# Two gated feed-forward branches: the hidden activations turned by 32x32 transposes on VectorE and 16 small transfers per block instead of by TensorE transposes

## The chip, the cores and the metric

The program runs on one core of one Trainium2 chip. The metric is the device time of one execution in microseconds (us); of several executions the median is given. "Engines" below are TensorE (PE in the rows; PEld is its weight load), VectorE (DVE), ScalarE (ACT), GpSimd (POOL) and SyncE (SP), which here only issues transfers.

## The reference, cut to what matters

One layer on x of 256 rows x 2048 columns, float32. Two gated feed-forward branches stand around a mixer; the change touches only the branches:

```python
def swiglu(h, w_gate, w_up, w_down):
    return (jax.nn.silu(h @ w_gate) * (h @ w_up)) @ w_down

h = modulate(rmsnorm(x, g_ffn1_pre[l]), sh1, sc1)
y = rmsnorm(swiglu(h, w1_gate[l], w1_up[l], w1_down[l]), g_ffn1_post[l])
x = x + MACARON_WEIGHT * gt1[:, None, :] * y
...
h = modulate(rmsnorm(x, g_mix_pre[l]), sh2, sc2)
y = hybrid_mixer(h, pos, ...)
x = x + gt2[:, None, :] * rmsnorm(y, g_mix_post[l])
...
```

The second branch is the same with its own weights. w_gate and w_up are 2048 x 5632, w_down is 5632 x 2048. The shifts, scales and gates (`sh1`, `sc1`, `gt1`, ...) are columns of `silu(c) @ w_ada + b_ada`, a matrix of 2048 x 18432 that is read once.

## The kernel before, in words

**Tiling.** The 256 rows are two tiles of 128 (`TT`). Every product is made with a float32r high part and a float32r low part of both factors: three matmuls (high by high, high by low, low by high; lines 1460 to 1462) for one. A *unit* is two 128-row chunks of a weight times 512 columns (512 KB): SP loads it into one of 8 `raw` buffers (line 430), ACT rounds it to `w_hi` (one of 4 buffers, line 565), DVE subtracts to `w_lo`, in the place of `raw` (line 924), and PE makes 12 matmuls of it.

**Gate and up.** The 5632 hidden columns are 11 blocks of 512 (`FB`). In a block PE makes 8 units of the gate and 8 of up, each into a PSUM pair. ACT takes silu of the gate into `s` (line 657), DVE multiplies `s` by the up product in place (`hidden`, line 1104). The down product contracts over hidden columns, so `s` has to be turned: PE makes eight 128x128 transposes in two fills of `tps` (`turn_s`, line 1543), behind unit 2 of the next block; ACT rounds each fill to `hid_hi` (`hi_hid`, line 663), DVE subtracts to `hid_lo` (`lo_hid`, line 1110). PE takes `hid_hi` and `hid_lo` only in the down product, after all blocks.

**The first four blocks of branch 1.** While the modulation columns come in, their products are built in four turns, and partial sums are kept. Only the last turn ends the blocks, so there a block has 4 units of PE work, not 16. ACT puts a partial sum back ahead of each product (`put_back`, line 731).

**Order.** Each engine has its program written out by hand: a loop over the units of a block, with the other work put in front of a given unit. In branch 1 DVE also adds up `w_ada` between the units (line 938), 12 instructions in a block of 16 units. Before the change the later blocks of the gate and up stand in hardware loops (`Fori`); `RUNS` says which. A `Fori` of several rounds there is in branch 2 alone (blocks 6 to 10).

**Waits.** ACT rounds unit u only when PE is done with unit u-4 (4 `w_hi` buffers). SP loads into a `raw` buffer when PE (a weight) or DVE (a piece of `w_ada`) is done with what lay there. In the short blocks ACT rounds two units ahead of the one at PE. GpSimd does nothing but four memsets at the start.

Of the kernel before, what the change touches and what calls it, by code (L numbers as in the profile page):

```python
# [24 lines left out]
ALU = mybir.AluOpType  # L25
ACT = mybir.ActivationFunctionType
# [93 lines left out]
def make_plan():  # L120
# [34 lines left out]
    for f in ("1", "2"):  # L155

        fills("mod" + f, 8 if f == "1" else 4, "a" if f == "1" else "va")
        fills("hid" + f, 2 * (FB - 1), "v")
        fills("gate" + f, 4, "a")
        fills("hidlast" + f, 2, "v")  # L160
# [12 lines left out]
def build(nc, A, const, out):  # L173
    pl, tp, taken, order = make_plan()
    ctx = ExitStack()
    with ctx:
# [87 lines left out]


# [41 lines left out]
        setup = sem("setup")  # L307

# [32 lines left out]
        def landed(r, i=0, per=0):  # L341

            extra = sum(q <= r and q % RING == r % RING for q in doubled)
            return 16 * (r // RING + 1 + extra) + (i * (16 * per // RING) if per else 0)

        def plus(n, i, per):

            return n + i * per if per else n
# [11 lines left out]
        for k, n in (("mod1", 8), ("hid1", 2 * FB), ("modmix", 8), ("qa", 2), ("kv", 1), ("mod2", 8), ("hid2", 2 * FB)):  # L360
            TH[k] = n_th
            n_th += n
# [4 lines left out]
        RUNS = {"gu1": [(b, 1) for b in range(OPEN_FF, FB)], "gu2": [(b, 1) for b in range(1, 6)] + [(6, FB - 6)]}  # L367
# [45 lines left out]

        block = ctx.enter_context(nc.Block())
# [3 lines left out]
        def _(sp):  # L418
            ada = A["w_ada"].rearrange("(p j) (q n) -> p j q n", j=KD, n=NB)

            def load(r, src, n=NB, i=0, per=0, per_w=0):

                if r >= RING:
                    before = r - RING
                    assert not per or order[before:r] == order[before + per:r + per]
                    if order[before] == "W":
                        sp.wait_ge(w_used, plus(order[:before + 1].count("W"), i, per_w))
                    else:
                        sp.wait_ge(raw_used, plus(before + 1, i, per))
                sp.dma_start(raw[:, r % RING, :, 0:n], src).then_inc(raw_landed[r % RING], 16)  # L430

            def stream(b, unit, i=0, per=0, per_w=0):

                for n, (kind, u) in enumerate(b.seq):
                    if kind == "W":
                        src, cols = unit(u)
                        load(b.r + n, src, cols, i, per, per_w)
# [46 lines left out]
            for f, gu, down in (("1", "gu1", "down1"), ("2", "gu2", "down2")):  # L484
# [6 lines left out]
                for start, count in RUNS[gu]:  # L491
                    b = pl[gu][start]
                    if count == 1:
                        stream(b, gate_up(wg, wu, start))
                        continue
                    with sp.Fori(0, count) as i:
                        stream(b, gate_up(wg, wu, i + start), i, len(b.seq), 16)
# [55 lines left out]

        @block.scalar
        def _(act):
            def hi_unit(b, u, i=0, per=0, per_w=0, n=NB):

                r, w = b.r_of(u), b.w + u
                act.wait_ge(raw_landed[r % RING], landed(r, i, per))
                if per or w >= HI_RING:  # L560
                    act.wait_ge(w_used, plus(w - HI_RING + 1, i, per_w))
# [1367 lines left out]
```

## Time and profile before

| | |
|---|---|
| runs | 1884.14, 1884.9 and 1886.74 us; median 1884.9 us |
| profiled execution, its span | 1881.6 us; no other time of it is given |
| PE busy | 1847.5 us (98% of the span) |
| DVE busy | 1317.3 us (70%) |
| ACT busy | 895.2 us (48%) |
| POOL busy | 0.2 us |
| HBM read | 485.04 MB |

The span is read from the first instruction to the last. What lies around it is the 3.3 us between the span and the median of the runs. A busy share is an average over the whole program. PE's matmuls are pipelined: a matmul of 512 columns lasts 0.39 us in a row but starts 0.227 us behind the one before it, and it is the distance of starts that counts.

### The profile page before, as it was taken

To read this page: it belongs to the slowest core of one execution; us is meant where nothing else is said; L and a number is where in the kernel's file an instruction comes from. 1 tells how busy PE (TensorE), PEld (TensorE's weight loads), DVE (VectorE), ACT (ScalarE), POOL (GpSimd) and SP (SyncE) were. 2 spreads that over 40 slices of the span, in tenths; PEclk is the share of its full clock that TensorE was granted. 3 is DMA by queue.
4 is the path that set the end of the run, shared out by engine and by line. 5 is a ranking of instruction groups with operands and counts; after the bars stand their busy time and mean duration, and the time that the engine had idled before them with its cause. 6 is when DMAs were issued, how large, how long until landed. Compare 5 with 4: busy or idle time off the path is not lost.

```text
span 1881.6 us, 23558 instructions
## 1 busy us (share of the span) xinstructions
PE 1847.5 (98%) x9016; PEld 1558.3 (83%) x9016; DVE 1317.3 (70%) x1394; ACT 895.2 (48%) x1145; POOL 0.2 (0%) x4
## 2 busy tenths in 40 slices
PE   6999999999999999999999999999999999999998
PEld 6888888888877888899988888887888888888886
DVE  5998888888878888788665768877554444444444
ACT  4678544344444344654447456444444444434443
POOL 0000000000000000000000000000000000000000
PEclk9999999999999999999999999999999999999999
DMA  9998899999989999678881775988666666555553
GB/s 375 407 395 272 284 325 327 332 328 333 325 286 323 334 328 333 213 245 263 283 262 56 231 240 186 312 280 285 199 190 185 188 189 185 179 194 195 191 192 132
DMA packets 236385, 488.56 MB, mean 260 GB/s; under 512 B 21638, under 2 KB 32252, under 8 KB 236028
## 3 DMA queue, kind: packets, MB, share of 16 engines
q1 hardware_dynamic: 235408, 486.67, 76.9%
q8 instruction: 65, 1.06, 0.2%
q10 hardware_dynamic: 876, 0.53, 0.1%
q14 instruction: 36, 0.29, 0.0%
HBM read 485.04 MB, written 2.10 MB: 259 GB/s over the span
## 4 chain that ended last, share of the span: by engine, by line
PE 91%; DVE 3%; DMA 3%; ACT 1%; DVEq 1%; issue 0%; SPq 0%; ACTq 0%
PE pair L1460 27%; PE pair L1462 27%; PE pair L1461 27%; PE pair L1509 2%; PE pair L1512 2%; PE pair L1511 2%; PE tps L1543 2%; DMA start_raw<-in_w_ada 1%; DVE start_acc L966 1%; DMA raw<-in_w_down 1%; DVEq L965 1%; DVE w_lo L924 1%; PE mps L1581 1%; DVE x L1140 1%; ACT w_hi L565 0%
## 5 line engine op out<-in xcount | busy, mean ns | idle before, releaser
L565 ACT ACTIVATE w_hi<-raw 128x1024 fp32r<-128x1024 f32 x634 | 668.1, 1056 | 877.9 <-PE pair L1462 397.3
L924 DVE TENSOR_TENSOR w_lo<-raw,w_hi 128x1024 fp32r<-128x1024 f32 x634 | 769.1, 1218 | 430.6 <-ACT w_hi L565 426.9
L1460 PE MATMUL pair<-w_hi,h_hi 128*128 128x512 f32 (+1 forms) x1656 | 645.7, 390 | 3.9 <-DVE w_lo L924 2.6
L1462 PE MATMUL pair<-w_hi,h_lo 128*128 128x512 f32 (+1 forms) x1656 | 642.3, 388 | 0.0
L1461 PE MATMUL pair<-w_lo,h_hi 128*128 128x512 f32 (+1 forms) x1656 | 641.9, 388 | 0.0
L1460 PEld LDWEIGHTS pair<-w_hi,h_hi 128*128 128x128 f32 x1656 | 310.9, 188 | 67.3 <-DVE w_lo L924 2.2
L1462 PEld LDWEIGHTS pair<-w_hi,h_lo 128*128 128x128 f32 x1656 | 310.8, 188 | 63.8
L1461 PEld LDWEIGHTS pair<-w_lo,h_hi 128*128 128x128 f32 x1656 | 311.0, 188 | 62.3
L938 DVE SCALAR_TENSOR_TENSOR acc<-raw,c_col,acc 128x1024 f32<-128x1024 f32 x210 | 269.8, 1285 | 32.4 <-DMA raw<-in_w_ada 14.3
L1460 PE MATMUL pair<-w_hi,hid_hi 128*128 128x512 f32 x704 | 274.9, 390 | 1.5 <-DVE w_lo L924 1.5
L1461 PE MATMUL pair<-w_lo,hid_hi 128*128 128x512 f32 x704 | 274.0, 389 | 0.0
L1462 PE MATMUL pair<-w_hi,hid_lo 128*128 128x512 f32 x704 | 273.9, 389 | 0.0
L1460 PEld LDWEIGHTS pair<-w_hi,hid_hi 128*128 128x128 f32 x704 | 132.1, 188 | 30.9 <-DVE w_lo L924 3.4
L1462 PEld LDWEIGHTS pair<-w_hi,hid_lo 128*128 128x128 f32 x704 | 132.1, 188 | 27.4
L1461 PEld LDWEIGHTS pair<-w_lo,hid_hi 128*128 128x128 f32 x704 | 132.2, 188 | 27.1
L966 DVE SCALAR_TENSOR_TENSOR start_acc<-start_raw,c_col,start_acc 128x1024 f32<-128x1024 f32 x55 | 70.7, 1285 | 15.4 <-DMA start_raw<-in_w_ada 10.4
L1509 PE MATMUL pair<-h_hi,w_hi 128*128 128x256 f32 x256 | 72.8, 284 | 0.3 <-DVE w_lo L924 0.3
L1512 PE MATMUL pair<-h_hi,w_lo 128*128 128x256 f32 x256 | 72.4, 283 | 0.0
L1511 PE MATMUL pair<-h_lo,w_hi 128*128 128x256 f32 x256 | 72.4, 283 | 0.0
L1509 PEld LDWEIGHTS pair<-h_hi,w_hi 128*128 128x128 f32 x256 | 49.1, 192 | 0.5 <-issue 0.5
L1511 PEld LDWEIGHTS pair<-h_lo,w_hi 128*128 128x128 f32 x256 | 49.1, 192 | 0.0
L1512 PEld LDWEIGHTS pair<-h_hi,w_lo 128*128 128x128 f32 x256 | 49.1, 192 | 0.0
(211 smaller groups left out, 869.9 us busy)
## 6 DMA issues: line engine op xcount, KB each, us to landing
raw<-in_w_ada SPq DMA_DIRECT2D x224, 512.0 KB, 4.3
raw<-in_w_gate SPq DMA_DIRECT2D x176, 512.0 KB, 4.6
raw<-in_w_up SPq DMA_DIRECT2D x176, 512.0 KB, 4.4
raw<-in_w_down SPq DMA_DIRECT2D x176, 512.0 KB, 4.2
start_raw<-in_w_ada SPq DMA_DIRECT2D x64, 512.0 KB, 8.9
raw<-in_w_in SPq DMA_DIRECT2D x56, 512.0 KB, 4.7
raw<-in_w_o SPq DMA_DIRECT2D x32, 512.0 KB, 4.7
raw<-in_w_uq SPq DMA_DIRECT2D x12, 256.0 KB, 4.4
```

The lines of the kernel that those rows point to most:

```text
L565: nc.scalar.activation(w_hi[:, w % HI_RING, :, 0:n], raw[:, r % RING, :, 0:n], ACT.Copy).then_inc(hi_ready, 1)
L924: nc.vector.tensor_tensor(w_lo[:, r % RING, :, 0:n], raw[:, r % RING, :, 0:n], w_hi[:, w % HI_RING, :, 0:n], ALU.subtract).then_inc(raw_us ...
L938: ins = nc.vector.scalar_tensor_tensor(into, raw[:, r % RING], c_col[:, 1, j:j + 1], into, ALU.mult, ALU.add)
L965: dve.drain()
L966: ins = nc.vector.scalar_tensor_tensor(total, tile, c_col[:, 1, j:j + 1], total, ALU.mult, ALU.add)
L1460: nc.tensor.matmul(o, hi, wh, start=first and kk == 0, stop=False, skip_group_check=added)
L1461: nc.tensor.matmul(o, hi, wl, start=False, stop=False, skip_group_check=added)
L1462: ins = nc.tensor.matmul(o, lo, wh, start=False, stop=last and kk == 1, skip_group_check=added)
L1509: nc.tensor.matmul(o, wh, hi, start=first and kk == 0 and c % 2 == 0, stop=False, skip_group_check=True)
L1511: nc.tensor.matmul(o, wh, lo, start=False, stop=False, skip_group_check=True)
L1512: ins = nc.tensor.matmul(o, wl, hi, start=False, stop=last and kk == 1, skip_group_check=True)
L1543: ins = nc.tensor.transpose(tps[0:rows, n % 2, k * P:(k + 1) * P], src, ident)
```

## The change

The hidden columns are turned without PE. DVE multiplies as before, then turns every 32x32 square of `s` in place of its own into `turned_s` (two instructions per block, one per row tile). GpSimd's queue then moves the squares between groups of 32 partitions: 4 x 4 transfers of 32 partitions x 1 KB (32 KB), from `turned_s` to `hid_raw`. ACT rounds `hid_raw` to `hid_hi`, DVE subtracts to `hid_lo`. Both new tensors lie in `y[:, 0, :]`, which is free in the branches. There is one `turned_s` and one `hid_raw`: GpSimd waits for `hid_ready` of block m-1 before the transfers of block m, and DVE makes `lo_hid` of block m-1 ahead of the transposes of block m. ACT's silu of a block waits until `s` of the block before has been turned.

```diff
+        @block.gpsimd
+        def _(pool):
+            for m in range(2 * FB):
+                pool.wait_ge(s_turned, m + 1)
+                if m:
+                    pool.wait_ge(hid_ready, m)
+                for b in range(NQ):
+                    for q in range(NQ):
+                        pool.dma_start(hid_raw[b * BLK:(b + 1) * BLK, q],
+                                       turned_s[q * BLK:(q + 1) * BLK, b]).then_inc(hid_landed[m // FB], 16)
...
-            def hi_hid(t0, c0, i=0, per_t=0):
-                for k in range(2):
-                    act.wait_ge(t_full, plus(t0 + k + 1, i, per_t))
-                    nc.scalar.activation(hid_hi[:, bass.ds(c0 + 2 * k, 2), :],
-                                         tps[:, (t0 + k) % 2, :].rearrange("p (c t) -> p c t", c=2),
-                                         ACT.Copy).then_inc(t_hi, 1)
+            def hi_hid(m):
+
+                act.wait_ge(hid_landed[m // FB], 16 * NQ * NQ * (m % FB + 1))
+                for t in range(TT):
+                    ins = nc.scalar.activation(hid_block(hid_hi, m, t), hid_part(t), ACT.Copy)
+                ins.then_inc(hid_rounded, 1)
...
                 elif at % 2 == 0:
-                    t0 = tp["hid1"] + at
-                    if at:
-                        hi_hid(t0 - 2, (at // 2 - 1) * 4)
-                    silu(pl["gu1"][at // 2], t_prev=t0 if at else None, w=2)
+                    if at > 2:
+                        hi_hid(at // 2 - 2)
+                    silu(pl["gu1"][at // 2], before=at // 2 - 1 if at else None, w=2)
...
+                m0 = FB * (f == "2")
+                for start in LATER[gu]:
+                    b = pl[gu][start]
+                    for u in range(16):
+                        if f == "1" and start == OPEN_FF and u == 3:
+                            hi_hid(start - 2)
+                        if u == 12:
+                            silu(b, before=m0 + start - 1)
+                        if u == 13:
+                            hi_hid(m0 + start - 1)
+                        hi_unit(b, u)
...
+                if between is not None:
+                    between()
+                dve.drain()
+                for t in range(TT):
+
+                    ins = nc.vector.transpose(turned_s[:, :, t],
+                                              s[:, t, :].rearrange("p (c b i) -> p b c i", c=DB, b=NQ))
+                ins.then_inc(s_turned, 1)
...
+                def last_open(n=n):
+                    hidden(pl["gu1"][n - 1], (lambda: lo_hid(n - 2)) if n > 1 else None)
+                run(b, {3: last_open} if n else None, start=0 if n else 1)
...
+                    def last_block(start=start):
+                        if f == "1" and start == OPEN_FF:
+                            lo_hid(start - 2)
+                        hidden(pl[gu][start - 1])
+
+                    def last_hidden(start=start):
+                        lo_hid(m0 + start - 1)
+                    run(pl[gu][start], {4: last_block, 14: last_hidden})
...
-                if turn == 3 and at % 2 == 0 and at:
-                    pe.wait_ge(evac[1], v // 2)
-                    turn_s(tp["hid1"] + at - 2)
```

PE waits for `hid_ready` ahead of the down product, and again at its unit 20 for the last block. The last block's `hi_hid` and `lo_hid` stand at units 13 and 14 of the first down block. The `Fori` loops of all engines are written out.

DVE's program from the last unit of short block 0 on. Before (the first `s<-s,pair` is the product of block 0, the second that of block 1):

```order
L1104 TENSOR_TENSOR s<-s,pair 128x512 x2
L924 TENSOR_TENSOR w_lo<-raw,w_hi 128x1024
L1110 TENSOR_TENSOR hid_lo<-tps,hid_hi 128x512 x2
L924 TENSOR_TENSOR w_lo<-raw,w_hi 128x1024 x2
L938 SCALAR_TENSOR_TENSOR acc<-raw,c_col,acc 128x1024
L924 TENSOR_TENSOR w_lo<-raw,w_hi 128x1024
L1104 TENSOR_TENSOR s<-s,pair 128x512 x2
L924 TENSOR_TENSOR w_lo<-raw,w_hi 128x1024
```

The same place in the changed kernel (`y<-s` is the transpose into `turned_s`, `hid_lo<-y` the subtraction of `hid_raw`):

```order
L1123 TENSOR_TENSOR s<-s,pair 128x512 x2
L1130 STREAM_TRANSPOSE y<-s 128x4x128 x2
L943 TENSOR_TENSOR w_lo<-raw,w_hi 128x1024 x3
L957 SCALAR_TENSOR_TENSOR acc<-raw,c_col,acc 128x1024
L943 TENSOR_TENSOR w_lo<-raw,w_hi 128x1024
L1123 TENSOR_TENSOR s<-s,pair 128x512 x2
L1138 TENSOR_TENSOR hid_lo<-y,hid_hi 128x4x128 x2
L1130 STREAM_TRANSPOSE y<-s 128x4x128 x2
L943 TENSOR_TENSOR w_lo<-raw,w_hi 128x1024
```

The subtraction of block 0 has moved from behind the next weight unit to between the multiplication and the transposes of block 1, ahead of the `w_lo` of that block's last unit.

ACT's program from the last rounded weight unit of short block 2 on, with its waits. Before (`s<-pair` is silu of block 2, `hid_hi` the rounding of block 1, `pair<-part` the partial sums put back):

```order
L565 ACTIVATE w_hi<-raw 128x1024 [waits w_used,raw_landed3]
L663 ACTIVATE hid_hi<-tps 128x512 [waits t_full] x2
L657 ACTIVATE s<-pair 128x512 [waits t_full,w_used]
L657 ACTIVATE s<-pair 128x512
L731 ACTIVATE pair<-part 128x512 x2
L565 ACTIVATE w_hi<-raw 128x1024 [waits w_used,raw_landed5]
```

The same place in the changed kernel:

```order
L583 ACTIVATE w_hi<-raw 128x1024 [waits w_used,raw_landed3]
L682 ACTIVATE hid_hi<-y 128x4x128 [waits hid_landed1]
L682 ACTIVATE hid_hi<-y 128x4x128
L675 ACTIVATE s<-pair 128x512 [waits s_turned,w_used]
L675 ACTIVATE s<-pair 128x512
L749 ACTIVATE pair<-part 128x512 x2
L583 ACTIVATE w_hi<-raw 128x1024 [waits w_used,raw_landed5]
```

The rounding in this place is now that of block 0, not of block 1, and it waits for the block's 16 transfers (`hid_landed1` counts those of branch 1); silu behind it waits for DVE's transposes of block 1.

## Rows read from the trace of the kernel before

**Rows 1.** The chain of work that ended last: shares of the span by engine.

```profile
PE 91%; DVE 3%; DMA 3%; ACT 1%; DVEq 1%; issue 0%; SPq 0%; ACTq 0%
```

**Rows 2.** Two stretches: length, busy time by engine, granted clock, DMA share, GB/s.

```profile
0.00:200.00 200.00, 183.75 (x864) 155.46 (x865) 162.52 (x163) 137.75 (x201) 0.20 (x4) 1.00 0.97 357
200.00:400.00 200.00, 199.93 (x906) 165.58 (x905) 171.90 (x161) 88.61 (x100) 0.00 (x0) 1.00 0.94 323
```

**Rows 3.** PE in order of time, transposes in branch 1: start, length, instruction, count.

```profile
363.55 0.39 PE L1462 MATMUL pair<-w_hi,h_lo 128*128 128x512 f32 x1
...
364.57 0.48 PE L1460 MATMUL pair<-w_hi,h_hi 128*128 128x512 f32 x1
...
364.89 0.40 PE L1461 MATMUL pair<-w_lo,h_hi 128*128 128x512 f32 x1
```

**Rows 4.** PE in order of time, end of branch 1's last block.

```profile
535.56 1.14 PE L1543 MATMUL tps<-cst,g_col 128*128 128x128 f32 x8 [0.25 <-ACT y L670]
...
536.99 1.06 PE L1543 MATMUL tps<-cst,s 128*128 128x128 f32 x8 [0.29 <-ACT y L670]
...
537.81 0.48 PE L1460 MATMUL pair<-w_hi,hid_hi 128*128 128x512 f32 x1
```

**Rows 5.** DVE, groups by line: count, busy us and mean ns, idle before.

```profile
L1104 DVE TENSOR_TENSOR s<-s,pair 128x512 f32<-128x512 f32 x44 | 28.1, 680 | 4.5 <-PE pair L1462 4.5
L1110 DVE TENSOR_TENSOR hid_lo<-tps,hid_hi 128x512 fp32r<-128x512 f32 (+1 forms) x44 | 28.2, 683 | 10.2 <-ACT hid_hi L663 10.2
L952 DVE STREAM_TRANSPOSE acc<-acc 128x512 f32<-128x512 f32 x28 | 19.9, 712 | 3.5 <-DMA raw<-in_w_ada 1.0
L924 DVE TENSOR_TENSOR w_lo<-raw,w_hi 128x1024 fp32r<-128x1024 f32 x634 | 769.1, 1218 | 430.6 <-ACT w_hi L565 426.9
L935 DVE TENSOR_SCALAR acc<-raw,c_col 128x1024 f32<-128x1024 f32 x14 | 10.4, 746 | 0.0
```

**Rows 6.** Transfer issues on ACT's queue at the start; then issues with size and landing.

```profile
0.73 0.43 ACTq L706 DMA_DIRECT2D c_col<-in_c  x1
...
4.53 0.36 ACTq L714 DMA_DIRECT2D fz<-in_b_forget  x1
...
c_col<-in_c ACTq DMA_DIRECT2D x1, 8.0 KB, 2.2
```

**Rows 7.** DVE and ACT in order of time, short blocks of branch 1.

```profile
189.54 1.28 DVE L1104 TENSOR_TENSOR s<-s,pair 128x512 f32<-128x512 f32 x2
...
201.65 1.22 DVE L924 TENSOR_TENSOR w_lo<-raw,w_hi 128x1024 fp32r<-128x1024 f32 x1
...
204.99 1.06 ACT L663 ACTIVATE hid_hi<-tps 128x512 fp32r<-128x512 f32 x2
```

**Rows 8.** PE, first matmul of units 59, 63 and 67 (weights counted from 0).

```profile
207.38 0.39 PE L1460 MATMUL pair<-w_hi,h_hi 128*128 128x512 f32 x1
...
219.18 0.39 PE L1460 MATMUL pair<-w_hi,h_hi 128*128 128x512 f32 x1
...
230.86 0.48 PE L1460 MATMUL pair<-w_hi,h_hi 128*128 128x512 f32 x1
```

**Rows 9.** A long block of branch 1: product on DVE, unit 13 on ACT and PE.

```profile
361.13 1.28 DVE L1104 TENSOR_TENSOR s<-s,pair 128x512 f32<-128x512 f32 x2
...
386.92 1.06 ACT L565 ACTIVATE w_hi<-raw 128x1024 fp32r<-128x1024 f32 x1 [0.86 <-DMA raw<-in_w_up]
...
391.87 0.39 PE L1460 MATMUL pair<-w_hi,h_hi 128*128 128x512 f32 x1
```

**Rows 10.** A block of branch 2: product on DVE, unit 13 on PE.

```profile
1455.27 1.28 DVE L1104 TENSOR_TENSOR s<-s,pair 128x512 f32<-128x512 f32 x2
...
1489.12 0.39 PE L1460 MATMUL pair<-w_hi,h_hi 128*128 128x512 f32 x1
```

**Rows 11.** DMA queues: packets, MB, share of 16 engines.

```profile
q1 hardware_dynamic: 235408, 486.67, 76.9%
```

More of the change, by code:

```diff
@@ L339, in build, with landed @@
         doubled = [b.r_of(u) for b in pl["uq"] + pl["ukv"] for u in range(b.nw)]
-        def landed(r, i=0, per=0):
+        def landed(r):
             extra = sum(q <= r and q % RING == r % RING for q in doubled)
-            return 16 * (r // RING + 1 + extra) + (i * (16 * per // RING) if per else 0)
-        def plus(n, i, per):
-            return n + i * per if per else n
+            return 16 * (r // RING + 1 + extra)
         N_X0, N_Y1, N_X1, N_QA, N_KV, N_YM, N_XM, N_Y2 = 0, 1, 3, 4, 5, 6, 8, 9
@@ L365, in build @@
         N_ATT = 2 * HEADS
-        RUNS = {"gu1": [(b, 1) for b in range(OPEN_FF, FB)], "gu2": [(b, 1) for b in range(1, 6)] + [(6, FB - 6)]}
+        LATER = {"gu1": range(OPEN_FF, FB), "gu2": range(1, FB)}
         def start_weight(w):
@@ L419, in _, with load, stream @@
             ada = A["w_ada"].rearrange("(p j) (q n) -> p j q n", j=KD, n=NB)
[L421 removed]
+            def load(r, src, n=NB):
                 if r >= RING:
                     before = r - RING
[L425 removed]
                     if order[before] == "W":
[L427 removed]
+                        sp.wait_ge(w_used, order[:before + 1].count("W"))
                     else:
[L429 removed]
+                        sp.wait_ge(raw_used, before + 1)
                 sp.dma_start(raw[:, r % RING, :, 0:n], src).then_inc(raw_landed[r % RING], 16)
[L432 removed]
+            def stream(b, unit):
                 for n, (kind, u) in enumerate(b.seq):
@@ L1463, in tile_products, with unit @@
                 return ins
-            def unit(b, u, lhs_hi, lhs_lo, k0, g, first, last, i=0, per=0, per_w=0, n=NB, added=False):
-                pe.wait_ge(raw_used, plus(b.r_of(u) + 1, i, per))
+            def unit(b, u, lhs_hi, lhs_lo, k0, g, first, last, n=NB, added=False):
+                pe.wait_ge(raw_used, b.r_of(u) + 1)
                 for t in range(TT):
@@ L1569, in turn_ahead @@
                     ins.then_inc(turned, 1)
-            def turn_s(n, free=True):
-                for k in range(2):
-                    transposes(n + k, [s[:, t, c * P:(c + 1) * P] for c in (2 * k, 2 * k + 1) for t in range(TT)], free)
             def start_tile(tile, j, first, last):
@@ L1626, in gate_rows, with gate_up @@
                     transposes(t0 + j, [g_col[:, k:k + 1].to_broadcast([P, P]) for k in range(4 * j, 4 * j + 4)])
-            def gate_up(b, i=0, per=0, per_w=0, per_g=0, ready=None, after=None, ahead=None):
+            def gate_up(b, ready=None, ahead=None):
                 for u in range(16):
@@ L1639, in gate_up @@
                         pe.wait_ge(h_ready, ready + u + 1)
-                    unit(b, u, h_hi, h_lo, 2 * (u % 8), g, u % 8 == 0, u % 8 == 7, i, per, per_w)
-                    if after is not None and u == 2:
-                        after()
+                    unit(b, u, h_hi, h_lo, 2 * (u % 8), g, u % 8 == 0, u % 8 == 7)
             pe.wait_ge(c_ready, 1)
```

138 lines of the change are left out of this document (59 added, 79 removed).

## The prediction, made before the changed kernel ran

> **What bounds the kernel now.** I read the chain of waits first: PE holds 91% of it [rows 1]. Then the stretches: from 200 to 400 us PE is busy 199.93 of 200 us at a granted clock of 1.00, the upper of its two levels, DVE 171.90 us (86%), and the DMA engines have a share of 0.94 at 323 GB/s [rows 2]. So the loads come as fast as PE takes them. What leaves PE's queue is gained in full, as long as nothing else arrives late; what comes late by more than the units prepared ahead of PE is lost in full. Last, PE in order of time around its transposes: how much of its queue they hold [rows 3].
>
> **What goes.** Starts of matmuls of one group lie 0.227 us apart. Around the eight transposes of `s` the starts are 363.55 and 364.57, 1.02 us, which is 0.79 too much, and the next distance, to 364.89, is 0.32 where 0.23 is usual: 0.09 more [rows 3]. That is 0.88 us per block, and 20 of the 22 blocks are like this: 17.7 us. In the two blocks before a down product the eight stand behind the gate's transposes: the last of those begin at 535.56, those of `s` at 536.99 behind a wait of 0.29, the products at 537.81 [rows 4]. Without them the products can begin about 1.1 us earlier: 2.2 us for two. **Together -19.9 us.** ACT's rounding and DVE's subtraction stay, with other operands; I leave them at their present 1.06 us [rows 7] and 2 x 0.68 us, rounded to 1.28 together as they overlap [rows 5].
>
> **What comes on DVE.** Two transposes per block, 0.71 us each by the nearest row, the transpose of a 128x512 tile [rows 5]: 1.42 us. In branch 2 DVE has time for it. In a long block of branch 1 it has 28 pieces of work in 44 us and is 86% busy [rows 2]; 1.42 us in 43.5 makes that 89 to 90%. PE does not wait for an average, but a `w_lo` may now be late once a block. Bounds: 0, and 1.42 us for each of 7 blocks, 10 us. I take 2 us, nearer to nothing, since the next units catch up.
>
> **The price that decides: D**, the time from the transposes of a block to the landing of its 16 transfers. GpSimd has no transfer in the trace. Nearest rows: ACT's queue issues eight small transfers between 0.73 and 4.89 us, 0.52 us each, and one of 8 KB lands 2.2 us after its issue [rows 6]. Lower end: 16 issues at 0.52 and one landing, D = 10.5. Upper end: no issue begins before the one before has landed, 16 x 2.2 = 35. Between them I take 1.0 us per issue, about the geometric mean and twice the hardware queue's, because nothing requires the transfers to wait for each other but another engine makes them: **D = 16 x 1.0 + 2.2 = 18.2**. The Trainium skill (DMA: Bandwidth & Descriptors, SWDGE vs HWDGE vs iDMA) says that transfers from GpSimd's queue have their descriptors computed in software; its section on latency gives about 1 us to the first byte against 0.6. By 16 times that 1 us D would be 18 as well; no row here shows it.
>
> **Where D is covered, and where not.** In a long block of branch 1 the product begins at 361.13; with 1.28 and 1.42 us `s` is turned at 363.8. ACT comes to unit 13, where it now waits for the landing, at 386.92: 23 us later. PE takes that unit at 391.87 and needs 1.06 (rounding), 1.06 (ACT's unit) and 1.22 (DVE's) before [rows 5, 7, 9]: PE waits if D is over 24.7, or 23.8 when the 0.88 us of the transposes is gone. In branch 2 the same sum from 1455.27 to 1489.12 gives 27.8 [rows 10]. At D = 18.2 both are free.
>
> The short blocks are different: 4 units, 10.9 us of PE each, and every block's transposes wait for the landing of the block before. I follow the times of the trace:
> - Block 0: product at 189.54, turned at 192.3, landed 192.3 + 18.2 = 210.5. ACT was free for it at about 205.
> - ACT rounds (1.06), DVE subtracts (1.28), DVE transposes block 1 (1.42) to 214.3; only then `w_lo` of unit 59 (1.22): 215.5. It ended at 202.9 before, behind the product [rows 7]. PE takes unit 59 at 207.38, less two pauses 205.6 [rows 8]: **9.9 us late.**
> - Block 1 lands at 232.5; the same 5.0 us: `w_lo` of unit 63 at 237.5. PE wants it at 219.18 less three pauses plus 9.9 = 226.4: **11.1 more.**
> - Block 2 was turned at 236.3 and lands at 254.5. Now ACT waits in front of unit 67: 1.06 + 1.06 + 1.22 make 257.9. PE wants it at 230.86 less four pauses plus 21.0 = 248.3: **9.6 more.**
> - In front of unit 68 DVE has the subtraction, the product and the transposes, 3.98 us, and `w_lo`, 1.22; PE gives it 2.72: **2.5 more.**
>
> Together 33.1 us, and 3 us for each further us of D. Behind that nothing is short of time, so PE does not win it back.
>
> **At no cost:** the 32 KB transfers on the DMA engines. They bring 352 x 32 = 11,264 packets of 1 KB beside 235,408, which took 76.9% of 16 engines [rows 11]: at most 98 ns each, 3 us of each engine in a long block. The loads of branch 1 need 28 x 0.524 MB in 43.5 us = 337 GB/s, with the transfers 349, and 357 are reached in the first 200 us [rows 2]. If this cover fails, loads land later and PE waits in branch 1 by some tenths per block. The loops written out: PE loses nothing at the loops' edges in the stretches I looked at, so there is nothing to win; the code grows a little.
>
> **Sum:** -19.9 + 2 + 33.1 = +15.2 us. The profiled span is 1881.6; with the 3.3 us around it that is the median of the runs, 1884.9, and the sum gives **1900**.
>
> **The rivals.**
> - *The queue is quick* (the other side). Issues at 0.52 us: D = 10.5. Then block 0 lands at 202.8, before ACT is there (204.1 with a pause less). The chain gives 3.6, 3.4, 1.9 and 2.5 us, 11.4 together, and 1884.9 - 19.9 + 11.4 = 1876. For it: the ACT queue's row; each transfer is only 32 pieces. Against: software in place of hardware. It decides below D = 14 (20 us lost), 0.74 us per issue. Chance 0.26.
> - *Between*, D near 14 (0.67 to 0.8 us per issue): within 4 us of before. Chance 0.12.
> - *Forecast*: D from 15 to 23, 1888 to 1915. Chance 0.50.
> - *The queue is held up*, D over 24. GpSimd would have to wait for DVE, which in branch 1 is nearly always in an instruction of about 1.2 us [rows 2, 5]: half of one per issue makes 1.6 us, D = 27.8. The short blocks then lose 33.1 + 3 x 9.6 = 61.9, seven long blocks 4.0 each, 28, branch 2 nothing: 1884.9 - 17.9 + 90 = about 1957. Against: most of these instructions are the subtraction of two tensors, and the quick form (1024 elements in 0.746 us) occurs 14 times in all [rows 5]. The Trainium skill (SBUF — State Buffer, Who interferes with whom) says that DVE's two-port forms lock GpSimd out for a whole instruction, descriptor writing included, but that a subtraction of two SBUF tensors takes only the read side; by that rule this case would hardly occur. No row here shows it. Chance 0.12.
>
> **How the numbers follow.** 0.2% (3.8 us) is about what a measurement of this kernel can tell from no change. Faster 0.27, within 0.2% 0.12, slower 0.61. The range runs from the quick queue's 1876 to 1.45 us per issue, D = 25.4: -19.9 + 2 + 33.1 + 3 x 7.2 = 36.8, and 1.6 in each of seven long blocks, 11.2, make 1933. What is left out is the lower part of the quick case and the held-up one. The likeliest case's own range is 1888 to 1915.
>
> **What would show it.** In the changed profile: POOL's queue with 16 issues of about 1 us in a row per block; ACT waiting for the transfers, for 8 to 20 us each, three times between 200 and 270 us, and nowhere else; PE idle about 10 us three times there, behind `w_lo`; from 300 us on, block for block 43.5 us where it was 44.4. It is wrong if an issue costs under 0.74 us (then faster), if ACT waits at unit 13 in the long blocks (D over 23), or if PE stalls in branch 1 by DVE or loads.

## The result and the profile after

The changed kernel takes 1892.1 us (median of 9 runs, 1886.6 to 1894.7) beside 1885.1 us of the kernel before on the same chip (9 runs): a ratio of 1.003, 95% interval 1.0018 to 1.0042, that is 3.4 to 7.9 us slower. Measured again later (12 runs) it gave 1887.2 beside 1885.6 us, ratio 1.0012, 1.0002 to 1.0022. Slower, then, as forecast, but by 2 to 6 us and not by 15. The profiled execution took 1892.17 us, its span is 1890.4 us, 8.8 more than the span before.

The page of the changed kernel, engines and then groups; the groups' columns are those of [rows 5], and the last two lines give the DMA queue and the landing:

```profile
PE 1841.1 (97%) x8840; PEld 1548.6 (82%) x8840; DVE 1341.8 (71%) x1438; ACT 895.5 (47%) x1145; POOL 172.4 (9%) x356
...
PE 86%; DMA 5%; DVE 4%; ACT 2%; DVEq 1%; issue 1%; POOL 1%; SPq 0%; ACTq 0%
...
q0 software_dynamic: 11264, 11.56, 2.0%
...
y<-y POOLq DMA_DIRECT2D x352, 32.0 KB, 3.7
```

PE's share of the last chain fell from 91% [rows 1] to 86%. The transfers take 2.0% of the DMA engines, and a transfer lands 3.7 us after its issue.

Groups of DVE and POOL:

```profile
L568 POOL DMA_DIRECT2D y<-y x352 | 172.2, 497 | 1483.3 <-DVE y L1130 1419.6 <-issue 63.7
...
L1130 DVE STREAM_TRANSPOSE y<-s 128x512 f32<-128x512 f32 x44 | 28.7, 691 | 2.1
L1138 DVE TENSOR_TENSOR hid_lo<-y,hid_hi 128x512 fp32r<-128x512 f32 x44 | 28.3, 685 | 12.2 <-ACT hid_hi L682 12.2
```

**An issue on GpSimd's queue costs 0.497 us**, where I took 1.0. The transposes cost 0.69 us and the subtraction 0.685, as [rows 5] said. POOL also stood still for 63.7 us "on issue", with nothing in the profile to wait for. Where, its order in time shows (start, length, count, idle before):

```profile
196.51 7.96 POOL L568 DMA_DIRECT2D y<-y  x16 [196.07 <-DVE y L1130]
214.80 2.44 POOL L568 DMA_DIRECT2D y<-y  x5 [10.33 <-DVE y L1130]
218.97 5.39 POOL L568 DMA_DIRECT2D y<-y  x11 [1.73 <-issue]
232.87 4.88 POOL L568 DMA_DIRECT2D y<-y  x10 [8.51 <-DVE y L1130]
239.52 2.95 POOL L568 DMA_DIRECT2D y<-y  x6 [1.77 <-issue]
253.67 7.32 POOL L568 DMA_DIRECT2D y<-y  x15 [11.21 <-DVE y L1130]
265.69 0.50 POOL L568 DMA_DIRECT2D y<-y  x1 [4.70 <-issue]
```

The queue pauses behind the 21st, 42nd and 63rd transfer, and so on every 21; in branch 2, which has its own semaphore, the count starts anew. The semaphore updates of the trace show what ends a pause. The 21st transfer lands at 218.41 and the 22nd is issued at 218.97; in all 16 such pauses the next issue begins 0.56 us behind the landing of the last transfer issued before it. So the queue stands until everything that it has issued has landed. ACT in the same stretch:

```profile
210.66 1.13 ACT L682 ACTIVATE hid_hi<-y 128x512 fp32r<-128x512 f32 x2
...
228.71 1.15 ACT L682 ACTIVATE hid_hi<-y 128x512 fp32r<-128x512 f32 x2 [3.15 <-DMA y<-y]
...
246.23 1.15 ACT L682 ACTIVATE hid_hi<-y 128x512 fp32r<-128x512 f32 x2 [9.64 <-DMA y<-y]
```

Block 1 is turned at 214.50 (the transposes begin at 213.21 and last 1.30) and rounded from 228.71 on: 0.3 + 16 x 0.497 + 1.73 + 4.3 = 14.2 us (the start of the first issue, 16 issues, the pause, and the time from the last issue's end to ACT's start). Block 2: 13.7. **In the short blocks D is 14, not 18.2.** For block 0 ACT does not wait for the landing (no idle time stands before it). In no long block does ACT wait.

PE at units 59, 63, 67 and 68, to be read with [rows 8]:

```profile
215.67 0.80 PE L1491 MATMUL pair<-w_hi,h_hi 128*128 128x512 f32 x1 [5.69 <-DVE w_lo L943]
...
219.86 0.39 PE L1491 MATMUL pair<-w_hi,h_hi 128*128 128x512 f32 x1
...
233.74 0.80 PE L1491 MATMUL pair<-w_hi,h_hi 128*128 128x512 f32 x1 [5.12 <-DVE w_lo L943]
...
249.64 0.50 PE L1491 MATMUL pair<-w_hi,h_hi 128*128 128x512 f32 x1 [2.24 <-DVE w_lo L943]
...
254.54 0.50 PE L1491 MATMUL pair<-w_hi,h_hi 128*128 128x512 f32 x1 [1.89 <-DVE w_lo L943]
```

The matmuls behind the two longest waits last 0.80 us instead of 0.39, and unit 60 begins 4.19 us behind unit 59, where a unit takes 2.72. The stretches say why (columns as in [rows 2]; the last is the only other such place, in branch 1):

```profile
215.60:218.90 3.30, 3.23 (x8) 2.61 (x9) 3.21 (x4) 2.19 (x4) 1.64 (x4) 0.55 0.18 50
...
232.50:239.00 6.50, 5.26 (x12) 4.13 (x13) 5.27 (x6) 3.92 (x5) 4.88 (x10) 0.50 0.27 85
...
331.50:334.50 3.00, 3.00 (x9) 2.33 (x8) 2.91 (x4) 0.78 (x1) 0.00 (x0) 0.50 0.55 200
```

The granted clock is at its lower level, 1.2 GHz, behind PE's waits of 5.69 and 5.12 us, and not behind those of about 2 us at units 67 and 68. In the second profile of this kernel it also fell at unit 67, behind a wait of 3.68 us. The forecast had no term for that.

From such starts of matmuls I made one table, for this kernel and those below: how much later than in the kernel before the first matmul of a unit begins, in us. Unit 0 is the first of all, 69 follows the short blocks, 176 is the first of branch 1's down product, 192 lies in it, 350 is in the first eighth of branch 2, 506 is the first of branch 2's down product. Behind branch 1 only units multiplied by line 1491 (1460 before) are counted, so 350 and 506 leave out those of the mixer that another line multiplies.

| kernel | unit 0 | 59 | 63 | 67 | 69 | 95 | 176 | 192 | 350 | 506 |
|---|---|---|---|---|---|---|---|---|---|---|
| changed | 3.8 | 8.3 | 14.6 | 18.8 | 21.0 | 21.9 | 20.0 | 19.6 | 19.0 | 8.6 |
| changed, again | 2.7 | 5.9 | 12.3 | 16.8 | 19.1 | 19.9 | 15.2 | 14.2 | 15.4 | 6.2 |
| straight | -0.1 | -0.2 | -0.2 | -0.2 | -0.2 | -0.3 | -0.2 | -1.6 | -1.6 | -2.1 |
| short8 | -0.2 | 1.8 | 4.8 | 9.2 | 12.0 | 13.6 | 11.0 | 10.0 | 9.5 | -1.6 |
| short1 | -0.2 | 1.8 | 4.9 | 4.2 | 5.2 | 6.6 | 5.1 | 4.1 | 6.3 | -4.9 |
| early | -0.6 | 11.4 | 26.6 | 38.8 | 41.0 | 42.0 | 36.5 | 35.0 | 35.5 | 25.2 |
| sem2 | -0.3 | 3.0 | 7.5 | 9.5 | 13.3 | 13.6 | 9.6 | 8.2 | 8.8 | -2.1 |
| small | 0.3 | 3.9 | 10.2 | 14.5 | 18.3 | 18.9 | 14.2 | 12.6 | 12.4 | 4.3 |
| long1 | -0.6 | 2.6 | 8.9 | 13.4 | 17.2 | 17.2 | 13.9 | 12.2 | 11.9 | 0.7 |
| halves | -0.2 | 4.0 | 10.0 | 14.7 | 17.1 | 29.8 | 45.3 | 43.6 | 43.1 | 35.1 |
| warm | -0.2 | 3.4 | 9.1 | 16.2 | 19.6 | 20.5 | 19.1 | 18.1 | 16.8 | 7.9 |
| sooner | -0.2 | 3.0 | 8.1 | 11.0 | 14.8 | 15.4 | 26.4 | 25.0 | 26.7 | 15.5 |
| two | 3.1 | 1.8 | 3.3 | 2.5 | 3.1 | 5.4 | 1.5 | 0.0 | -0.1 | -11.3 |
| best | 0.2 | -1.4 | -1.3 | -2.1 | -1.7 | 2.8 | -0.2 | -2.0 | -0.7 | -11.2 |
| best2 | 2.7 | 1.1 | 1.6 | 0.8 | 1.6 | 2.3 | 2.3 | 1.5 | 0.8 | -9.4 |

### The profile page after: what moved, and what is told of

Read it like the earlier page. It is cut to its first block, busy times and chain, and to the rows that moved or that the text cites. A ratio compares the mean times of both kernels' runs of the same rounds, so it can differ in the third digit from the quotient of the medians.

```text
span 1890.4 us, 23049 instructions
## 1 busy us (share of the span) xinstructions
PE 1841.1 (97%) x8840; PEld 1548.6 (82%) x8840; DVE 1341.8 (71%) x1438; ACT 895.5 (47%) x1145; POOL 172.4 (9%) x356
## 4 chain that ended last, share of the span: by engine, by line
PE 86%; DMA 5%; DVE 4%; ACT 2%; DVEq 1%; issue 1%; POOL 1%; SPq 0%; ACTq 0%
PE pair L1491 25%; PE pair L1493 25%; PE pair L1492 25%; PE pair L1543 2%; PE pair L1540 2%; PE pair L1542 2%; DMA raw<-in_w_up 1%; DMA raw<-in_w_down 1%; DVE w_lo L943 1%; DMA start_raw<-in_w_ada 1%; PE tps L1574 1%; POOL y L568 1%; DVE acc L957 1%; PE mps L1608 1%; ACT w_hi L583 1%
## 5 line engine op out<-in xcount | busy, mean ns | idle before, releaser
L568 POOL DMA_DIRECT2D y<-y x352 | 172.2, 497 | 1483.3 <-DVE y L1130 1419.6
```

The costliest lines, as they stand in the source:

```text
L568: pool.dma_start(hid_raw[b * BLK:(b + 1) * BLK, q], turned_s[q * BLK:(q + 1) * BLK, b]).then_inc(hid_landed[m // FB], 16)
```

## The experiments

Ratios are to the kernel before on the same chip, with the 95% interval.

### The loops written out, alone: straight

```diff
-                    with act.Fori(0, count) as i:
+                    with written_out() as i:
```

(`written_out()` returns `nullcontext(0)`; the same on SP, DVE and PE, with one round per block)

> The kernel before with its loops written out and nothing else changed. Theory (the written-out loops cost nothing, and the 3.8 us by which the changed kernel is late at its first product are chance of the clock's first rise): 1883 to 1887 us, the same as before, and the first unit of products begins about 39 us after the span's start. Rival (longer code costs PE or the start something in every execution): 1888 to 1890, with the clock's first rise near 45 us instead of 32.

Measured: 1884.2 us, ratio 1.0005 (0.9994 to 1.0016); unit 0 begins as before. The loops are worth nothing that can be measured.

### Fewer transfers in the short blocks: short8, short1

```diff
+                        if b * NQ + q >= KEEP(m):
+                            continue
                         pool.dma_start(hid_raw[b * BLK:(b + 1) * BLK, q],
```

(`KEEP(m)` is 8, or 1, for m < 3 and 16 otherwise; ACT waits for as many)

> The changed kernel with 8 of the 16 transfers of each of the first three blocks left out (half of the turned values of those blocks is missing). Theory (the time from the transposes to the landing, D, sets the loss in the short blocks, 3 us for each us of D down to about 10.5, less below): D falls from 14 to 4 + 3.7 = 7.7, the chain of three landings shrinks by 10 to 14 us, about 1880 us. Rival (what is lost there is DVE's and ACT's added work in a fixed order, or the clock): under 4 us of gain, 1888 or more.

> The changed kernel with 15 of the 16 transfers of each of the first three blocks left out. Theory: D is about 4.2, nobody waits for a landing, and what is left of the loss is the order on DVE in front of units 63, 67 and 68: 14 to 17 us of gain on the changed kernel, about 1877. If the gain stops at that of eight transfers, DVE's own chain is the floor. Rival (not the transfers): 1888 or more.

Measured: 1882.3 us, 0.9998 (0.9984 to 1.0012); and 1879.8 us, 0.9981 (0.9970 to 0.9992). The time lies in the landings: from unit 0 to 69 the changed kernel loses 17.2 us, with 8 transfers 12.2, with one 5.4. With 8 that is 5.0 us less where I expected 10 to 14, since a pause of 4.95 us fell into block 2's eight issues, and ACT waited 9.8 us there. With one it is 11.8 us less where I expected 14 to 17. Of the 5.4 us left, 2.0 are lost at unit 59 (before the landing of any block is waited for), the rest behind it, and PE waits for w_lo each time (3.36, 1.89 and 0.83 us). I put that down to DVE's order, with the subtraction, the product and the transposes in one piece; the kernel with two buffers, below, has the same work on DVE in another order and loses none of it.

### More in the short blocks: early

```diff
-                        pool.dma_start(hid_raw[b * BLK:(b + 1) * BLK, q],
...
+                        if m >= OPEN_FF - 1:
...
+                            continue
+                        for t in range(TT):
+                            pool.dma_start(hid_raw[b * BLK:(b + 1) * BLK, q, t],
```

(under the `if` stands the transfer as it was)

> The changed kernel with each transfer of the first three blocks made as two of 16 KB, the long blocks as they were. Theory (each us of D costs 3 us in the short blocks; an issue costs 0.5 us whatever it moves): D = 32 x 0.5 + 3.3 and one or two pauses of 2 to 5 us = 22 to 26 instead of 14, so 24 to 36 us slower than the changed kernel, ratio 1.016 to 1.022. Rival (the loss per us flattens because fewer units wait): under 20 us, ratio under 1.013.

Measured: 1910.9 us, 1.0140 (1.0125 to 1.0154), 24 us above the changed kernel measured beside it (1887.2), at the lower edge of what was expected (24 to 36 us, ratio from 1.016). ACT now waits three times:

```profile
213.70 1.15 ACT L687 ACTIVATE hid_hi<-y 128x512 fp32r<-128x512 f32 x2 [9.89 <-DMA y<-y]
240.72 1.15 ACT L687 ACTIVATE hid_hi<-y 128x512 fp32r<-128x512 f32 x2 [12.10 <-DMA y<-y]
266.23 1.15 ACT L687 ACTIVATE hid_hi<-y 128x512 fp32r<-128x512 f32 x2 [17.62 <-DMA y<-y]
```

D is 22.1, 23.2 and 21.6 us (turned at 191.6, 217.6, 244.6). Beside the changed kernel blocks 1 and 2 land 9.0 and 7.9 us later after their turning, block 0 by 7.7 (ACT is there at about 206 otherwise): 24.6, and PE is 24.4 us later at unit 69 than with D = 14 (41.6 from unit 0 on, against 17.2). One us of each landing is one us of the kernel, 3 us per us of D as forecast.

### The pauses of the queue: sem2

```diff
-        hid_landed = [sem(f"hid_landed{f}") for f in (1, 2)]
+        hid_landed = [[sem(f"hid_landed{f}{k}") for k in range(2)] for f in (1, 2)]
...
-                                       turned_s[q * BLK:(q + 1) * BLK, b]).then_inc(hid_landed[m // FB], 16)
+                                       turned_s[q * BLK:(q + 1) * BLK, b]).then_inc(hid_landed[m // FB][m % FB % 2], 16)
...
-                act.wait_ge(hid_landed[m // FB], 16 * NQ * NQ * (m % FB + 1))
+                act.wait_ge(hid_landed[m // FB][m % FB % 2], 16 * NQ * NQ * (m % FB // 2 + 1))
```

> The changed kernel with the landings counted on two semaphores in turn (by the parity of the block); buffers, waits and order as they were. In the changed kernel GpSimd pauses 1.7 to 5.7 us after every 21st transfer; with two semaphores and two buffers the pauses were 0.2 us after every 16th. Theory (the pauses hang on the semaphore, and those of blocks 1 and 2, 1.73 and 1.77 us, stood in D one for one): 3 to 4 us faster, ratio about 1.001, D = 12.2. Rival (the pauses went because the second buffer gave more room in time): pauses as in the changed kernel, ratio 1.003.

Measured: 1883.4 us, 1.0000 (0.9986 to 1.0013). POOL in order of time:

```profile
209.54 2.45 POOL L568 DMA_DIRECT2D y<-y  x5 [9.36 <-DVE y L1130]
212.19 5.40 POOL L568 DMA_DIRECT2D y<-y  x11 [0.20 <-issue]
...
290.60 5.39 POOL L568 DMA_DIRECT2D y<-y  x11 [0.20 <-issue]
```

The pauses are gone but for 0.20 us, once behind the 21st transfer and then once per 16, with nothing changed but which semaphore counts a landing. At 212.19 the queue goes on although the last of the transfers before lands only at 213.16. The other pause of 2 to 5 us per block in the long blocks went too. D is 12.4 and 11.5. Unit 69 begins 13.6 us later after unit 0 than in the kernel before; in the first profile of the changed kernel it was 17.2, in the five others that have the same program up to about there it was 16.4 (again), 18.0 (small), 17.8 (long1), 17.3 (halves) and 15.0 (sooner), so the gain is 1.4 to 4.4 us. The time alone does not tell sem2 from the second measurement of the changed kernel (1.0002 to 1.0022).

That the pause is a wait for all landings holds in every kernel here with one semaphore per branch: each such pause ends 0.55 or 0.56 us behind the last landing. It comes behind 21 transfers with 16 KB as with 32 KB; why 21 is open. The Trainium skill (DMA: Bandwidth & Descriptors, Why a DMA increments its semaphore by 16 and not by 1) asks for one semaphore per slot in flight so that a count cannot pass early; no run here shows a count that did.

### The long blocks: small, long1, halves

small cuts each of the two transposes of six long blocks to one 32x32 square; long1 leaves out 15 of 16 transfers of seven long blocks (`KEEP(m)` is 1 for `3 <= m < 10`); halves is early with the test turned round, so that the long blocks have 32 transfers.

```diff
+                    if small:
+                        ins = nc.vector.transpose(turned_s[:, 0, t, 0], s[:, t, 0:BLK])
+                        continue
```

> The changed kernel with the two transposes of six long blocks of branch 1 cut to one 32x32 piece each (their turned values are missing). Theory (DVE's added 1.4 us per long block is what makes w_lo late there, and keeps back 0.5 to 0.9 us per block of what PE gained): 3 to 6 us faster than the changed kernel, ratio to before about 1.001, and the unit starts of branch 1 fall back by 0.9 us per block as in branch 2. Rival (the load on the DMA engines, or what the stalls before left behind): no gain, ratio about 1.003.

> The changed kernel with 15 of the 16 transfers left out in seven long blocks of branch 1 (m = 3 to 9; most of their turned values are missing). Rival (16 transfers of 32 KB per block on top of a DMA share of 0.94 delay the loads of branch 1): 3 to 6 us faster than the changed kernel, ratio about 1.001. Theory (it is DVE's work): no gain, ratio about 1.003.

> The changed kernel with each transfer of the long blocks (m of 3 and up) made as two of 16 KB; the first three blocks as they were. Theory (an issue costs 0.5 us whatever it moves, so D in the long blocks is 32 x 0.5 + 5 + 3.7 = about 25; they hide D up to 23.8 in branch 1 and 27.8 in branch 2): ACT waits for a landing by 0 to 2 us in branch 1 and not in branch 2, 0 to 8 us slower than the changed kernel, ratio 1.003 to 1.007. Rival 1 (an issue costs by size): D under 20, no change. Rival 2 (the long blocks hide less than their slack says): over 10 us slower, ratio over 1.008.

Measured: small 1888.8 us, 1.0034 (1.0021 to 1.0047); long1 1884.5 us, 1.0009 (0.9996 to 1.0021); halves 1920.3 us, 1.0204 (1.0184 to 1.0224). By these times the transfers' load costs something and DVE's transposes nothing. But long1 is not apart from the changed kernel's second measurement (1.0012), nor small from its first (1.0030), and the traces don't separate them either: from unit 69 to 176 PE gains 4.1 us with small and 3.3 with long1, while kernels whose long blocks are as in the changed one gain 4.5 (early), 3.9 (again), 1.0 (the first profile), 1.0 (short8), 0.5 (warm) and 0.1 (short1). So this contrast stays inconclusive.

halves is clear, though outside all three expectations: over 10 us slower, as rival 2 said, but not because less is hidden. My price of D was too small. One block's issues and ACT:

```profile
296.78 1.96 POOL L573 DMA_DIRECT2D y<-y  x4 [25.81 <-DVE y L1135]
303.12 10.25 POOL L573 DMA_DIRECT2D y<-y  x21 [4.38 <-issue]
317.98 3.43 POOL L573 DMA_DIRECT2D y<-y  x7 [4.61 <-issue]
```

```profile
325.44 1.15 ACT L687 ACTIVATE hid_hi<-y 128x512 fp32r<-128x512 f32 x2 [7.75 <-DMA y<-y]
```

Two pauses fall into it, and 325.4 - 296.5 = 28.9 us pass from the turning to the rounding, 5.1 more than the 23.8 that the forecast gave as hidden. PE waits as long at the unit in question, unit 93:

```profile
328.84 0.50 PE L1496 MATMUL pair<-w_hi,h_hi 128*128 128x512 f32 x1 [4.98 <-DVE w_lo L948]
```

In the seven blocks D is 23.2 to 29.9 us. What it has above 23.8 adds up to 20.6 us, and at the unit 13 of these blocks PE falls back by 20.8 in all: the slack of branch 1 was forecast rightly. PE lost more than that. From unit 69 to 176 it lost 28.2 us, although the transposes that are gone give back 6.9; so some 14 us came behind those waits, where the changed kernel has 3 to 6. In the block shown unit 94 begins another 1.7 us late, at the lower granted clock (0.54 from 328.9 to 332.5), and units 95 and 96 another 3.3. How these 14 us are shared between the clock and DVE's order is not shown.

In branch 2 D stays under the 27.8 that are hidden (20.8 to 26.8). ACT does wait there, up to 6.1 us, which I had not expected, but no loss of PE is seen: from unit 350 to 506 it gains 8.0 us, the kernels with the usual transfers there 8.1 (small) to 11.2. An issue of 16 KB costs as much as one of 32 KB (0.496 us, median of both).

### The clock behind the waits: warm

```diff
+                    if turn == 3 and half == 1 and v % OPEN in (5, 7):
+                        keep_warm(28 if v % OPEN == 5 else 44)
```

(and 19 and 17 in front of units 67 and 68)

> The changed kernel with fillers on PE (28, 44, 19 and 17 transposes of the identity, 0.11 us each) in front of units 59, 63, 67 and 68, inside the waits for the landings. Theory (the granted clock falls to the lower level behind these waits, and units 59 and 63 then take 4.2 and 5.3 us instead of 2.7): no fall of the clock between 200 and 260 us, 3 to 4 us faster than the changed kernel, ratio about 1.001. Rival (the next unit waits for the same chain anyhow, so a slower clock costs nothing): no gain, ratio 1.003.

Measured: 1895.1 us, 1.0062 (1.0048 to 1.0076): slower than without the fillers. The granted clock stayed at 2.4 GHz until 246.8 us, and unit 59 took 2.9 us; but unit 63 came only 0.6 us sooner after unit 59 (17.5 us against 18.1), since what it waits for is the landing and not PE. The theory falls: in front of another landing the lower clock cost next to nothing. Where no landing follows it does cost: in the first profile of the changed kernel, in short1 and in best it falls behind unit 95, and unit 96 begins another 1.4 to 1.6 us late; in the eight other profiles with the subtraction at the same place and no fall there, 0.0 to 0.1. In the profile of warm block 2 landed 3 us later than usual, behind a pause of 3.6 us; the other runs of this kernel were slower still, up to 1901 us, which its one profile (1891.4) does not explain.

### Two buffers in turn: two, best

```diff
-                if m:
-                    pool.wait_ge(hid_ready, m)
+                i, k = m % FB, m % FB % 2
+                if m == FB:
+                    pool.wait_ge(hid_ready, m)
+                elif i > 1:
+                    pool.wait_ge(hid_ready, m - 1)
...
-                        pool.dma_start(hid_raw[b * BLK:(b + 1) * BLK, q],
+                        pool.dma_start(hid_raw[k][b * BLK:(b + 1) * BLK, q],
```

(k is the parity of the block; `hid_landed` as in sem2; rounding and subtraction of blocks 0 and 1 stand one block later)

> The changed kernel with the turned and the landed values in two places used in turn (by the parity of the block), so that the transposes of a block no longer wait for the landing of the block before; rounding and subtraction of the short blocks stand one block later. Theory: the 20 us of the short blocks come back but for DVE's work, which is the same and better spread: 1872 to 1877 us, faster than both. Rival (GpSimd's queue or its pauses in the short blocks hold the second half of them up all the same): 1883 to 1888.

best, in the long blocks:

```diff
-                    tasks = {4: last_block, 14: last_hidden}
+                    tasks = {4: last_block, 6: turn_last, 14: last_hidden}
```

> The kernel with two buffers, with two moves on DVE: in block 3 the product goes ahead of the subtraction of block 0 (PE stood 2.2 us there behind ACT's copy of a bank that the product frees), and in the long blocks the transposes stand at unit 6, the product at unit 4, so that no 2.6 us stand in one piece in front of w_lo. Theory (both sit on PE's path): 1 to 4 us faster than with two buffers alone, 1869 to 1872 us, ratio about 0.994. Rival (branch 1 is held by its loads, whatever DVE does): only the 1 us of the first move, ratio 0.995.

Measured: two 1872.4 us, 0.9951 (0.9934 to 0.9967), **faster than both kernels**; best 1873.4 us, 0.9943 (0.9931 to 0.9956), no different. From unit 0 to 69 two loses nothing, where the changed kernel lost 17.2 us; between units 59 and 69 PE waits 2.2 us at one bank and 0.4 for w_lo. best takes these 2 us (-1.9 at unit 69) but loses 4.5 us to unit 95, 2.6 of them at unit 95 itself, and 1.4 more at unit 96, at the lower clock; so its second move, the later transposes, brought nothing. The stretches of two:

```profile
200.00:260.00 60.00, 56.54 (x246) 45.48 (x245) 52.42 (x56) 32.31 (x41) 27.39 (x56) 1.00 1.01 336
260.00:400.00 140.00, 137.95 (x607) 113.34 (x606) 124.26 (x118) 58.59 (x63) 23.68 (x48) 1.00 0.96 340
```

The DMA engines are as good as full here (1.01, 0.96).

### The place of the subtraction: sooner, best2

In the first profile of the changed kernel PE is late at unit 95, by DVE:

```profile
322.12 1.29 DVE L1138 TENSOR_TENSOR hid_lo<-y,hid_hi 128x512 fp32r<-128x512 f32 x2
323.32 1.22 DVE L943 TENSOR_TENSOR w_lo<-raw,w_hi 128x1024 fp32r<-128x1024 f32 x1
324.63 1.29 DVE L957 SCALAR_TENSOR_TENSOR acc<-raw,c_col,acc 128x1024 f32<-128x1024 f32 x1
326.01 0.71 DVE L971 STREAM_TRANSPOSE acc<-acc 128x512 f32<-128x512 f32 x1
...
328.96 2.35 DVE L943 TENSOR_TENSOR w_lo<-raw,w_hi 128x1024 fp32r<-128x1024 f32 x2
```

The subtraction, which the change moved from unit 7 to unit 14, stands right before the row sums of `w_ada`.

```diff
-                        if u == 13:
+                        if u == (10 if f == "1" and start > OPEN_FF else 13):
                             hi_hid(m0 + start - 1)
...
-                    run(pl[gu][start], {4: last_block, 14: last_hidden})
+                    run(pl[gu][start], {4: last_block, (11 if f == "1" and start > OPEN_FF else 14): last_hidden})
```

> The changed kernel with ACT's rounding at unit 10 and DVE's subtraction at unit 11 of the long blocks of branch 1 after the first, instead of 13 and 14. In the changed kernel DVE's w_lo of unit 95 ends at 330.2 behind the subtraction (unit 94), a step of w_ada and its row sums, PE waits for it and the clock falls behind that wait. Theory (the subtraction's new place costs 1.3 us there, and the fall of the clock as much again): unit 95 no longer late, no fall of the clock near 330 us, between units 80 and 111 the kernel loses nothing or gains 0.9 us where it lost 0.1 to 1.4, span 1 to 3 us shorter than its own two profiles, ratio 0.999 to 1.001. Rival (the loads hold branch 1): no change, ratio 1.001 to 1.003.

> The kernel with two buffers, with the product ahead of the subtraction in block 3 and the same earlier subtraction in the long blocks of branch 1; the transposes stay at unit 4. Theory: 2 us from the first move (seen with the last kernel), 2 to 4 us from the second, 1867 to 1870 us, ratio about 0.992. Rival (loads): as with two buffers, ratio 0.9945 to 0.995.

Measured: sooner 1899.8 us, 1.0087 (1.0072 to 1.0101), far outside both; best2 1871.0 us, 0.9933 (0.9921 to 0.9945), the fastest of all but not apart from two and best. ACT in sooner:

```profile
352.82 1.15 ACT L682 ACTIVATE hid_hi<-y 128x512 fp32r<-128x512 f32 x2 [5.94 <-DMA y<-y]
...
400.81 1.15 ACT L682 ACTIVATE hid_hi<-y 128x512 fp32r<-128x512 f32 x2 [5.66 <-DMA y<-y]
```

These blocks were turned at 334.2 and 382.2: **in a long block with a pause in it D is 17.8 to 18.6 us** (four of the six moved); at unit 13 that is hidden, at unit 10 it is not. In the other two no pause falls between the transfers, and ACT does not wait at unit 10, 15.1 and 14.6 us behind the turning. With two semaphores, in best2, it waits in none of them, 13.6 to 15.2 us behind it. The subtraction's place does decide about unit 95: with it at unit 14 that unit falls behind unit 94 by 1.0 to 2.6 us (eleven profiles), at unit 11 by 0.6 and 0.5 (sooner, best2). But that is only a part of branch 1: by unit 176 two and best2 both stand near 2.

### Once more: again

> The changed kernel once more, unaltered, beside the three below. Theory (the late first rise of the clock, 44.5 us after the start instead of 32, with the first unit of products 3.8 us late, is chance: the kernels with the same start but fewer transfers did not show it): most likely a first unit at 38 to 39 us, a span of 1885 to 1887, ratio 1.002 to 1.004. Rival (it comes with this kernel): first unit at 42 us or later again.

The rival came out: the first unit was 2.7 us late again, and the clock rose late (below). It did so in two and best2 also, and in none of the other twelve profiles, ten of them of kernels with the same program as the changed one up to there. Whether it is chance stays open. The ratio, 1.0012, was below both ranges.

## Why the prediction was wrong in size, by its own steps

- **What goes (-19.9).** Held. In branch 2 the changed kernel gains 11.0 us from unit 192 to 506 (forecast 9.9). In branch 1 the starts come forward by 0.9 to 1.0 us where a long block's transposes stood and by 1.4 in front of the down product (forecast 0.88 and 1.1); in the short blocks the four pauses are part of the 17.2 below. 20 x 0.88 is 17.6, not 17.7.
- **The price of D: the step that failed.** "I take 1.0 us per issue, about the geometric mean and twice the hardware queue's": the measured issue is 0.497 us, just under the lower bound that the row of ACT's queue gave, 0.52 [rows 6]. "Twice" had no row behind it, and I should have stood nearer to that row. The other half of the term, one landing of 2.2 us, was too small: 3.7 us, and 4.3 until ACT starts. And a pause of 1.7 us was in no row. The three together make D = 14.2 instead of 18.2: 4 us too much, 12 us of time. The Trainium skill (DMA: Bandwidth & Descriptors, Anatomy of one DMA — SWDGE (gpsimd) path) gives 2.0 us plus the bytes at 436 GB/s for a transfer from GpSimd; my estimate from that is 2.1 us for 32 KB. The trace has 3.7.
- **Short blocks (33.1 at D = 18.2, 3 us per us).** The mechanism was right. With D = 14.2 the four steps of the forecast, less PE's pauses, are 4.1, 6.2, 4.7 and 2.5 us at units 59, 63, 67 and 69, together 17.5; the first profile has 4.5, 6.3, 4.2 and 2.2, together 17.2. The five other profiles with the same program up to there have 15.0 to 18.0. early confirms the slope (24.4 us for 24.6 us of later landings); with fewer transfers, in short8 and short1, the gain stops short of it.
- **Long blocks (2 us for DVE; hidden up to D = 23.8, and 27.8).** The slack was right: D was 18.6 at most in sooner, unseen at unit 13, and in halves PE's waits add up to what D had above 23.8. The 2 us were not: unit 69 to 176 should have given 6 x 0.88 + 1.1 - 2 = 4.4 us and gave 1.0 in the first profile and 3.9 in the second. Of the 5.9 us lost there in the first, 3.3 stand at units 95 and 96: PE waits 1.76 us for w_lo, by the subtraction's new place, and the clock falls behind it. Of the 2.9 lost in the second, 2.0 stand there. I did not price that place, though the diff shows it. How the rest is shared between DVE and the loads stays open; the earlier subtraction in best2 brought about 1 us at unit 95 and nothing measurable in the time.
- **Transfers on the DMA engines, at no cost.** They took 2.0% of the engines, 54 ns a packet, under the 98 ns taken as a bound. That this costs PE nothing is not shown: the times of long1 and small leave some us open.
- **Loops at nothing.** Held (straight).
- **The rivals.** What came is "between", D near 14: its time was within 4 us of before, which the second measurement gives but for its edge (0.4 to 4.1) and the first touches (3.4 to 7.9), and with a chance of 0.12 it had too little. By its bounds (0.67 to 0.8 us per issue) it would have been missed all the same: the issue was quick as in the first rival, and pause and landing made up for it. The held-up queue did not come. The quick rival's sum of 1876 and the limit of D = 14 leave out the 2 us for DVE that the forecast has; with them the limit is 18.2 - 15.2 / 3 = 13.1. The sign "an issue under 0.74 us, then faster" was wrong for the same reason: the issue cost 0.497 us and the kernel was slower.
- **The time and luck.** With D = 14.2 the forecast's own sum gives 1888. The first median, 1892.1, lies in the 1888 to 1915 of the likeliest case, but not by its mechanism: the profile has 3.8 us of a late first unit and 3 us more lost in the long blocks, neither of them in the sum.
- **Sum of the profile.** 3.8 (late first unit) + 17.2 - 1.0 - 0.4 - 0.6 - 10.4 = 8.6 us at unit 506, and 8.8 in the span.

## What to carry to other kernels

A chain "compute, many small transfers, wait" costs its whole length once per link wherever the block is shorter than the chain, and nothing where the block hides it; so find the slack of each stage before pricing the transfer, and give the first stages a second buffer and a second semaphore, which here turned 2 to 6 us of loss into 9 to 13 us of gain. A queue without a row in the trace is best priced like the most similar queue; here its issue was that near, and the landing and a pause came on top. When an edit moves an instruction within a block, look at what stands next to its new place, even if the block's average has room.

## What the runs showed of the hardware that I had not expected

- **The queue's pauses.** When one semaphore counts the landings of a branch, GpSimd pauses behind every 21st transfer until all that it has issued has landed, and 0.56 us more: 1.7 to 5.7 us in the changed kernel. When two take turns it pauses 0.2 us once per 16.
- **GpSimd and DVE's quick form.** In halves the issues are 0.496 us at the least and at the median, 0.926 at the most:

```profile
L573 POOL DMA_DIRECT2D y<-y x608: 496/496/926, 249.6 to 1688.7; - x152
```

```profile
268.66 0.74 DVE L959 TENSOR_SCALAR acc<-raw,c_col 128x1024 f32<-128x1024 f32 x1
```

The longest begins at 268.58, 0.08 us before DVE begins this instruction, the quick form of [rows 5], and ends 0.10 us behind it. All five issues above 0.6 us behind the first one of all lie over such an instruction, and each ends 0.10 us behind its end. Four more began 0.2 us or more before one and kept their 0.5 us, and so do the issues beside DVE's subtractions. The Trainium skill (SBUF — State Buffer, Who interferes with whom) says that a DVE instruction in a two-port form and GpSimd hold a shared pair of ports for a whole instruction and shut the other out, and that a subtraction of two SBUF tensors contends only with GpSimd's reads. The trace agrees with that, and with the small chance given to the held-up queue.
- **The first rise of the clock.** The granted clock rises to the higher level between 30.9 and 32.4 us in twelve profiles, and between 42.6 and 44.5 us in four (the changed kernel twice, two, best2). There the first matmul of unit 0 lasts 0.78 us and begins at 41.5 to 42.7 us, instead of 0.50 us at 38.8 in the kernel before. That is 2.7 to 3.8 us. The row of the first profile:

```profile
42.66 0.78 PE L1491 MATMUL pair<-w_hi,h_hi 128*128 128x512 f32 x1
```
